# A transformer trunk's differential attention: one combining pass on VectorE and a turning product by a scaled diagonal

## What is computed

```python
def diff_attend(q, k, v, lam):
    b, h2, nq, _ = q.shape
    s = jnp.einsum('bhqd,bhkd->bhqk', q, k).astype(jnp.float32)
    p = jax.nn.softmax(s, axis=-1).reshape(b, h2 // 2, 2, nq, k.shape[2])
    w = p[:, :, 0] - lam * p[:, :, 1]
    return jnp.einsum('bhqk,bhkd->bhqd', w.astype(v.dtype), v)
```

## Time and profile before

| | |
|---|---|
| runs | 2911.39, 2913.27, 2911.05 us |
| median | 2911.39 us |
| span of the profiled execution | 2899.9 us |
| median less this span | 11.5 us |
| PE busy | 2795.9 us, 96% |
| DVE, ACT, POOL busy | 1636.0 (56%), 809.6 (28%), 305.8 us (11%) |
| mean granted clock of PE | 0.983 |

### The profile page before, as it was taken

How to read it: one execution, slowest core, us unless ns; L and a number is a source line. 1 busy time by engine, 2 the same in 40 slices (tenths; PEclk the granted TensorE clock), 3 DMA queues, 4 the chain that set the end, 5 groups by cost and what they waited for, 6 DMA issues and landing times.

```text
span 2899.9 us, 40732 instructions
## 1 busy us (share of the span) xinstructions
PE 2795.9 (96%) x15252; PEld 2522.6 (87%) x15252; DVE 1636.0 (56%) x2849; ACT 809.6 (28%) x1091; POOL 305.8 (11%) x293
## 2 busy tenths in 40 slices
PE   7999999999988999999999999999999988999998
PEld 6999999989744789999999899999997844788887
DVE  4676577658747567756676772222236758533334
ACT  4221122132346332211221322112223256322222
POOL 0000000031337100000000000000003336000000
PEclk9999999999997999999999999999999999999999
DMA  6333333321221113332332232111212311222222
GB/s 227 132 124 114 115 116 132 114 74 66 55 50 31 45 67 121 127 120 106 126 134 98 91 120 76 55 59 65 72 52 88 76 35 36 73 94 102 87 101 80
DMA packets 64419, 265.02 MB, mean 91 GB/s; under 512 B 9024, under 2 KB 11968, under 8 KB 54848
## 3 DMA queue, kind: packets, MB, share of 16 engines
q1 hardware_dynamic: 52800, 188.56, 18.7%
q0 software_dynamic: 11520, 75.11, 7.7%
HBM read 252.89 MB, written 2.10 MB: 88 GB/s over the span
## 4 chain that ended last, share of the span: by engine, by line
PE 91%; DVE 5%; ACT 2%; issue 2%; POOL 0%; DMA 0%; SPq 0%; DVEq 0%; ACTq 0%; POOLq 0%
PE ps L1682 82%; PE ps L2025 1%; PE ps L2007 1%; DVE nmax L1490 1%; PE ps L1959 1%; PE ps L1948 1%; PE ps L1710 1%; PE ps L1991 1%; PE ps L1951 1%; PE ps L1943 1%; DVE w_lo L1114 1%; DVE y_lo L1198 1%; ACT probs_t L1017 0%; PE ps L1917 0%; ACT e_sb L1003 0%
## 5 line engine op out<-in xcount | busy, mean ns | idle before, releaser
L1682 PE MATMUL ps<-y_hi,w_hi 128*128 128x384 f32 (+2 forms) x3184 | 902.7, 348 | 33.2 <-DVE y_lo L1198 17.4
L1682 PE MATMUL ps<-y_hi,w_lo 128*128 128x384 f32 (+2 forms) x3184 | 893.6, 345 | 0.0
L1682 PE MATMUL ps<-y_lo,w_hi 128*128 128x384 f32 (+2 forms) x3184 | 893.3, 345 | 0.0
L1682 PEld LDWEIGHTS ps<-y_hi,w_hi 128*128 128x128 f32 x3184 | 579.7, 189 | 70.3 <-DVE y_lo L1198 22.7
L741 ACT ACTIVATE w_hi<-w_raw 128x1024 fp32r<-128x1024 f32 (+1 forms) x290 | 327.0, 1128 | 1066.4 <-PE ps L1682 1058.9
L1682 PEld LDWEIGHTS ps<-y_lo,w_hi 128*128 128x128 f32 x3184 | 583.6, 189 | 24.8
L1682 PEld LDWEIGHTS ps<-y_hi,w_lo 128*128 128x128 f32 x3184 | 583.3, 189 | 23.7 <-issue 0.2
L1114 DVE TENSOR_TENSOR w_lo<-w_raw,w_hi 128x1024 fp32r<-128x1024 f32 (+1 forms) x290 | 386.4, 1333 | 323.0 <-ACT w_hi L741 319.7
L1129 DVE SCALAR_TENSOR_TENSOR mod_acc<-mod_raw,cact,mod_acc 128x256 f32<-128x256 f32 x896 | 360.0, 477 | 0.0
L1682 PE MATMUL ps<-h_hi,w_hi 128*128 128x384 f32 (+2 forms) x1254 | 355.6, 343 | 0.0
L1682 PE MATMUL ps<-h_lo,w_hi 128*128 128x384 f32 (+2 forms) x1254 | 353.4, 342 | 0.0
(11 more groups left out here) (232 smaller groups left out, 1903.0 us busy)
## 6 DMA issues: line engine op xcount, KB each, us to landing
w_raw<-in_w_up SPq DMA_DIRECT2D x176, 512.0 KB, 3.2
mod_raw<-in_w_mod POOLq DMA_DIRECT2D x64, 1024.0 KB, 5.1
w_raw<-in_w_down SPq DMA_DIRECT2D x64, 704.0 KB, 4.0
w_raw<-in_w_in SPq DMA_DIRECT2D x36, 512.0 KB, 3.2
mod_start<-in_w_mod SPq DMA_DIRECT2D x8, 1024.0 KB, 18.2
w_raw<-in_w_out SPq DMA_DIRECT2D x16, 512.0 KB, 3.2
stack<-qk_hi SPq DMA_DIRECT2D x48, 96.0 KB, 2.1
band<-in_rpb POOLq DMA_DIRECT2D x16, 224.0 KB, 6.7
```

Of the source, the lines that this page charges most:

```text
L1682: mm = pe.matmul(slot[s][:, at:at + b - a], w[s][:, k, :], r[:, k, a:b], start=(opens and n == 0), stop=(closes and n == 2))
```

## The change

Three things change for differential steps; neighbourhood steps keep their arithmetic.

First, the combination. The weights are p0/sum0 - lam * p1/sum1. They are now written as (p0 + c * p1) / sum0 with c = -lam * sum0 / sum1. DVE forms c in `nrsum` and makes the bracket in one scalar_tensor_tensor over both halves. POOL's two passes go.

Second, the division by sum0 moves into the turning. POOL makes a 128x128 diagonal (the identity times 1/sum0), and PE turns a block by an ordinary matmul with the block as weight and the diagonal as moving operand, where it was a transpose by the identity. The two diagonals lie in a free end of `w_lo`.

Third, in every odd iteration k the turned probabilities of a differential step are copied out of PSUM by DVE, and not by ACT.

Waits follow these edits: the semaphore `first_scaled` becomes `diagonal`, and DVE and POOL wait for older diagonals and turned tiles before they overwrite what these were made from.

```diff
+    diagonal = [place(f"diagonal{s}", [P, P], at=at_lo + 4 * (s * FG + DC) * P) for s in range(2)]
...
                     t.wait("sums_inverted")
-                    factor = nrsum[:, e - 1:e] if kind == "diff" else rsum[:, e:e + 1]
-                    factor = factor.to_broadcast([P, keys.stop - keys.start])
-                    probs = probs_of(steps, k, 1)
-                    pool.tensor_tensor(probs[:, keys], probs[:, keys], factor, ALU.mult).then_inc(sems["half_scaled"], 1)
                     if kind == "diff":
 
-                        t.wait("first_scaled")
-                        pool.wait_ge(sems["half_scaled"], scores_before(layer) // 2 + k + 1)
-                        first = probs_of(steps, k, 0)
-                        pool.tensor_tensor(first[:, keys], first[:, keys], probs[:, keys], ALU.add).then_inc(sems["probs"], 1)
+
+                        if k >= n_na + 2:
+                            pool.wait_ge(sems["turned"], turned_before(layer) + 2 * n_na + k - n_na - 1)
+                        pool.tensor_tensor(diagonal[k % 2][:, :], ident[:, :], rsum[:, e - 1:e].to_broadcast([P, P]),
+                                           ALU.mult).then_inc(sems["diagonal"], 1)
+                    else:
+                        factor = rsum[:, e:e + 1].to_broadcast([P, keys.stop - keys.start])
+                        probs = probs_of(steps, k, 1)
+                        pool.tensor_tensor(probs[:, keys], probs[:, keys], factor, ALU.mult).then_inc(sems["half_scaled"], 1)
...
-                            if s == 0:
+                            if s == 0 and turned[0] == "diff" and k % 2:
+                                t.skip("turned")
+                            elif s == 0:
                                 copy_probs(k, turned[2][s])
...
+                        if k >= n_na + 2:
+
+                            dve.wait_ge(sems["diagonal"], diff_before(layer) + k - n_na - 1)
+                        dve.wait_ge(sems["half_scaled"], na_before(layer) + min(k - 1, n_na))
+                        dve.reciprocal(rsum[:, e0:e0 + 2], esum[:, e0:e0 + 2]).then_inc(sems["sums_inverted"], 1)
+                        t.wait("sums_inverted")
+                        dve.scalar_tensor_tensor(nrsum[:, e0:e0 + 1], rsum[:, e0 + 1:e0 + 2], lam[:, 5:6], esum[:, e0:e0 + 1],
+                                                 ALU.mult, ALU.mult).then_inc(sems["stat"], 1)
+                        t.wait("stat")
...
-                    ins = dve.tensor_scalar(first, first, rsum[:, e0:e0 + 1], None, ALU.mult)
-                    ins.then_inc(sems["first_scaled" if kind == "diff" else "probs"], 1)
+                    if kind == "diff":
+
+                        ins = dve.scalar_tensor_tensor(first, probs_of(steps, k, 1)[:, keys], nrsum[:, e0:e0 + 1], first, ALU.mult, ALU.add)
+                    else:
+                        ins = dve.tensor_scalar(first, first, rsum[:, e0:e0 + 1], None, ALU.mult)
+                    ins.then_inc(sems["probs"], 1)
...
                     m = turned_at(steps, k)
-                    if m is None or steps[m][0] != "na":
+                    if m is None or steps[m][0] != "na" and k % 2 == 0:
                         return
...
+                    if kind == "diff":
+                        t.wait("diagonal")
...
-                        mm = pe.transpose(turn[:, P * n_key:P * n_key + P], probs[:, P * key:P * key + P], ident[:, :])
+                        block = probs[:, P * key:P * key + P]
+                        if kind == "diff":
+                            mm = pe.matmul(turn[:, P * n_key:P * n_key + P], block, diagonal[k % 2][:, :], start=True, stop=True)
+                        else:
+                            mm = pe.transpose(turn[:, P * n_key:P * n_key + P], block, ident[:, :])
```

More of the change, by code:

```diff
@@ L240 @@
     "v_turned", "v_ready0", "v_ready1", "band_raw", "band_step", "band_ready",
-    "scores", "neg_max", "exp", "stat", "sums_inverted", "probs", "half_scaled", "first_scaled", "na_hi", "na_lo", "turned", "probs_t", "pv", "head_out",
+    "scores", "neg_max", "exp", "stat", "sums_inverted", "probs", "half_scaled", "diagonal", "na_hi", "na_lo", "turned", "probs_t", "pv", "head_out",
     "head_sq", "head_sum", "head_sqrt", "head_rstd", "head_norm", "final", "out_stored",
@@ L281, in trunk @@
     w_hi = [place(f"w_hi{s}", [P, FG, P], F32R) for s in range(2)]
+    at_lo = cursor[0]
     w_lo = [place(f"w_lo{s}", [P, FG, P], F32R) for s in range(2)]
+    diagonal = [place(f"diagonal{s}", [P, P], at=at_lo + 4 * (s * FG + DC) * P) for s in range(2)]
     at_mod = cursor[0]
@@ L464, in diff_scores, with na_before, diff_before @@
         return 2 * sum(s[0] == "diff" for s in attention_steps(layer < LAYERS - 1))
+    def na_before(layer):
+        return sum(na_scores(n) for n in range(layer)) // 2
+    def diff_before(layer):
+        return sum(diff_scores(n) for n in range(layer)) // 2
     def na_scores(layer):
@@ L678, in mixer @@
                 steps = attention_steps(layer < LAYERS - 1)
+                n_na = sum(step[0] == "na" for step in steps)
                 for k, (kind, h, tiles, ctx, last) in enumerate(steps):
@@ L1496, in invert_sums @@
                     t.wait("exp", 2)
[L1497 to L1506, removed]
+                    if k < n_na:
+                        if k >= 2 or layer:
+                            dve.wait_ge(sems["half_scaled"], na_before(layer) + max(k - 1, 0))
+                            if layer:
+                                dve.wait_ge(sems["diagonal"], diff_before(layer))
                         dve.reciprocal(rsum[:, e0:e0 + 2], esum[:, e0:e0 + 2]).then_inc(sems["sums_inverted"], 1)
                         t.wait("sums_inverted")
+                    else:
[7 more added lines that the diff above has]
+                        t.wait("stat")
                 def scale_probs(k):
@@ L1528, in copy_second @@
                     m = turned_at(steps, k)
-                    if m is None or steps[m][0] != "na":
+                    if m is None or steps[m][0] != "na" and k % 2 == 0:
                         return
                     kind, h, tiles, ctx, last = steps[m]
-                    q = tiles[1]
-                    dve.wait_ge(sems["turned"], turned_before(layer) + 2 * (m + 1))
+                    q = tiles[-1]
+                    dve.wait_ge(sems["turned"], turned_before(layer) + sum(len(step[2]) for step in steps[:m + 1]))
                     if jobs_before(layer) + jobs_by(with_ctx, k):
@@ L2019, in transpose_probs @@
                     else:
-                        pe.wait_ge(sems["half_scaled"], scores_before(layer) // 2 + k + 1)
+                        pe.wait_ge(sems["half_scaled"], na_before(layer) + k + 1)
+                    if kind == "diff":
+                        t.wait("diagonal")
                     if tiles_turned:
```

## The result

| | before | changed |
|---|---|---|
| median of the runs beside each other | 2911.22 us | 2947.84 us |
| lowest, highest | 2909.39, 2913.27 | 2944.14, 2948.92 |
| ratio | | 1.0117 (95% interval 1.0097 to 1.0136) |
| span of the profiled execution | 2899.9 us | 2946.4 us |

A forecast was written before the change was run, and what follows sets the result against it. It took TensorE as the bound, 96% busy, with DVE and GpSimd bounding steps without value products. +8.4 us in the second mixer and +6.8 in the first gave +15.2 on 2911.4: 2927 us, range 2914 to 2944.

The forecast's parts named there:

- The product's price: Turning of differential blocks on TensorE: 0.23 us a product against 0.125 us a transpose, +0.63 us for six blocks.
- it is off every path: GpSimd's diagonal, estimated at 0.4 us, holds up nothing, being wanted two steps later.
- The wait for the copy: Turning after odd steps waits for DVE's copy, 3.4 us from second scores; stalls of 0.47 and 1.4 us in second-mixer head.
- The four steps with no head products before them: Second mixer, before its first head: a pair of steps takes 7.8 us against 7.46, +0.7 us in all.
- come out even: First mixer, six turned steps before the first head: no time added when stepped at full clock.
- The ends: Last steps of each mixer, to the output product: +1 us in the first mixer, +2.7 us in the second.
- rival A: Stretches without value products stay at 1.2 GHz, 1.2 us more in some ten turned steps, +12: 2939 us; chance 0.22.
- Rival B: No stall on the copy, only TensorE's own work added in the 21 full steps: 2920 us; chance 0.20.
- Rival C: Product costs what the transpose did, DVE's scaling shrinks in steps without products: about -8, 2903 us; chance 0.05.
- Rival D: Turning blocks cost 0.50 us instead of 0.23, 56 us beyond the forecast: 2983 us; chance 0.03.
- rival E: Whole kernel: the terms cancel and nothing measurable changes, 2911 us; chance 0.05.
- The base: Whole kernel: 11.5 us between the 2899.9 us span and the 2911.39 us median lie outside the span, unchanged.

The follow-up runs named there:

- nodiag_act: Changed kernel with identity transposes, ScalarE copying and no diagonal made, division by the first sum left out: 2911.05 us, ratio 0.9994 to the kernel before.
- product_act: Changed kernel, but ScalarE copies every differential turned tile; product and vector pass stay: 2924.23 us, ratio 1.0041 to the kernel before.
- before_again: The kernel before, unchanged, executed and traced once more: span 2919.7 us against 2899.9 in its first trace.
- before_product: The kernel before, with differential blocks turned by a matmul with the identity in place of the transpose: 2923.27 us, ratio 1.0034 to the kernel before.
- transpose_dve: Changed kernel with identity transposes, division by the first sum left out, DVE still copying in odd steps: 2927.44 us, ratio 1.005 to the kernel before.
- transpose_act: Changed kernel with identity transposes and ScalarE copying, division left out, diagonal still made: 2911.84 us, ratio 0.9995 to the kernel before.
- copy_first: Changed kernel with DVE's copy of a differential tile placed ahead of the vector pass in the same iteration: 2928.68 us, ratio 1.0055 to the kernel before.

## Why the prediction was wrong

The direction was right and the size was not: +15.2 forecast, some +34 measured, outside the range. The prices of the instructions held. What failed is the stepping: it let DVE be free at the start of each pair of steps and took TensorE at full clock throughout, and so made the waits for the copy too small. By stretches, from one turning to a later one, in us:

| stretch | before | changed | more | forecast |
|---|---|---|---|---|
| first mixer, six steps before the first head | 19.6 | 24.7 | +5.1 | 0 |
| its first head | 20.9 | 25.2 | +4.3 | +2.9 |
| its second head | 25.4 | 28.9 | +3.5 | +2.9 |
| its last steps, to `mix_out` | 25.6 | 29.7 | +4.0 | +1 |
| second mixer, four steps before the first head | 14.7 | 17.6 | +3.0 | +0.7 |
| its first head | 15.3 | 19.2 | +3.9 | +2.5 |
| its second head | 17.6 | 22.3 | +4.8 | +2.5 |
| its last steps, to `mix_out` | 18.0 | 22.7 | +4.7 | +2.7 |
| sum | | | +33.3 | +15.2 |

Every stretch grew by more than forecast. Of the 18 us that are missing, 7.3 lie before the first heads, 5.7 in the heads and 5.1 at the ends. (The stage lengths above give 33.5 us, from edges in tenths.)

*The product's price* held: 0.23 us a block forecast, 1.43 / 6 = 0.24 measured, two records each and 416 in all. *The vector pass* held: 1.01 us. *The diagonal* held at 0.40 us, but "it is off every path" failed in part: GpSimd's instruction stretches DVE's factor instruction from 0.22 to 0.46 us where they meet (15 of 40 steps in the changed kernel), and nodiag_act puts the diagonal with its waits at about 4 us in all, not far above what two traces differ by.

*The wait for the copy* was the right mechanism, in the right places (wait after odd iterations), and too small. Where DVE was free the step nearly held: forecast from the start of the second scores 3.4 us, measured from 2453.77 to 2457.39: 3.62. So the stalls of 1.4 us in the second mixer's heads measured 1.46 and 1.45. The stalls of 0.47 at step 16 and its like in the second head measured 1.19 and 1.20, and the head that was to take 17.8 us took 19.2. The largest error is in the steps without value products: in the second mixer "The four steps with no head products before them", at 7.8 us a pair, and in the first mixer the six that "come out even". It is the same error as at step 16. I let each pair begin with an idle DVE. In the trace it is not idle. The timeline of DVE before the turning at 2446.83:

```profile
2440.58 0.96 DVE L1503 TENSOR_REDUCE nmax<-ps 128x1 f32<-128x768 f32 x1 [2.42 <-PE ps L1971]
2441.45 1.01 DVE L1536 SCALAR_TENSOR_TENSOR e_sb<-e_sb,nrsum 128x768 f32<-128x768 f32 x1
2442.38 0.95 DVE L1503 TENSOR_REDUCE nmax<-ps 128x1 f32<-128x768 f32 x1
2443.25 0.15 DVE L1523 RECIPROCAL rsum<-esum 128x2 f32<-128x2 f32 x1
2443.44 0.46 DVE L1525 SCALAR_TENSOR_TENSOR nrsum<-rsum,lam,esum 128x1 f32<-128x1 f32 x1
2443.93 0.96 DVE L1503 TENSOR_REDUCE nmax<-ps 128x1 f32<-128x768 f32 x1
2444.80 1.01 DVE L1536 SCALAR_TENSOR_TENSOR e_more<-e_more,nrsum 128x768 f32<-128x768 f32 x1
2445.73 0.95 DVE L1563 COPY probs_t<-ps 128x768 f32<-128x768 f32 x1
2446.60 0.95 DVE L1503 TENSOR_REDUCE nmax<-ps 128x1 f32<-128x768 f32 x1
```

From 2440.58 on, DVE has no gap: the second maximum of step 14 had to wait for scores behind the late turning, and all that follows runs on to the copy's end. The turning of PE at steps 11, 12, 14, 15 and 16 (iterations k, as in DVE's order above):

```profile
2423.20 1.50 PE L2052 MATMUL ps<-diagonal,e_sb 128*128 128x128 f32 x12
...
2428.83 1.58 PE L2052 MATMUL ps<-diagonal,e_sb 128*128 128x128 f32 x12 [1.44 <-DVE probs_t L1563]
...
2437.11 2.72 PE L2052 MATMUL ps<-diagonal,e_more 128*128 128x128 f32 x12 [1.80 <-DVE probs_t L1563]
...
2440.83 1.57 PE L2052 MATMUL ps<-diagonal,e_sb 128*128 128x128 f32 x12
...
2446.83 1.58 PE L2052 MATMUL ps<-diagonal,e_sb 128*128 128x128 f32 x12 [1.19 <-DVE probs_t L1563]
```

The loop is turning, second scores, maximum, pass, maximum, inversion, maximum, pass, copy, and turning again: 1.43 + 0.65 + 0.87 + 0.93 + 0.87 + 0.41 to 0.65 + 0.87 + 0.93 + 0.95 + 0.15, about 8.2 us, and 2437.11 - 2428.83 = 8.28. From 2437.11 to 2446.83 it is 9.72, with turning at half clock (2.38 us). Before, two such steps took 7.46. In the four steps before the first head of the second mixer this gave +3.0 us (2423.20 to 2440.83) where I had +0.7. The kernel before had:

```profile
2392.14 0.82 PE L2025 MATMUL ps<-ident,e_sb 128*128 128x128 f32 x6
...
2406.81 1.50 PE L2025 MATMUL ps<-ident,e_sb 128*128 128x128 f32 x6
```

In the first mixer, from turning at 878.14 to 902.83 against 874.26 to 893.90, it gave +5.05 where I had none; the granted clock in that stretch is 0.69.

*The ends* failed in two terms. In the first mixer I had stalls of 1.1 us and took off 1.6 for a wait on ScalarE's copy. The trace has waits for DVE's copy of 2.03 and 1.42 us there, the second in the place of the one that I took off. In the second mixer the turning that follows a 2 us wait is at half clock, 2.58 us to the next work, and so are the value products behind it, 3.17 instead of 1.86; the stall of 0.9 that I had there for the copy did not come:

```profile
964.20 1.58 PE L2052 MATMUL ps<-diagonal,e_more 128*128 128x128 f32 x12 [2.03 <-DVE probs_t L1563]
...
2482.32 2.93 PE L2052 MATMUL ps<-diagonal,e_sb 128*128 128x128 f32 x12 [2.03 <-ACT hid_buf L1072]
```

*The clock* (rival A) came in half. The 1.2 GHz stretches, which my sum left out, did not vanish: the stages' clocks are 0.87 and 0.95, up from 0.80 and 0.91. Turning at half clock takes 2.4 to 2.6 us, which rival A priced rightly at 1.2 us more; it happens in six turnings of six blocks, where rival A had some ten. There was luck in the price: its 0.43 us a block was read from products over 64 columns, and the blocks here have 128.

*Rival B* (no stall) is excluded by the waits for the copy, 17.4 us in 14 cases, and by product_act: without the copy the kernel is 20 us faster in the stages. *Rival C* (faster) is excluded by the records; its mechanism exists, since the steps without products did fall to 3.35 us, and was worth nothing in time. *Rival D* is excluded by 0.24 us a block, *rival E* by the interval of the ratio.

*The base* was wrong in a detail. I took 11.5 us as lying outside the span. The changed kernel's profiled execution took 2948.10 us with a span of 2946.4, and before_again 2921.42 with 2919.7, so 1.7 us lie outside. If that holds for the first trace of the kernel before, its execution was some 10 us shorter than the median (an estimate: its own time is not on record). This moved no term.

## What to carry to other kernels

An instruction that is moved to an engine with free time costs what stands ahead of it in that engine's queue. Where another engine waits for it, follow the loop over as many iterations as its waits reach (two, here), starting from the state in which the loop leaves the queues, and not from idle engines. The position can matter more than the engine: the same copy placed ahead of the pass gave back 15 of its 16 to 20 us. A turning product must be compared with the transpose it replaces by its records: in FP32 it was two for one here, and folding a scale into it is dear where TensorE is the bound.

## What the runs showed of the hardware

- An FP32 product of a 128x128 weight with 128 columns leaves two records and takes 0.24 us at 2.4 GHz, the transpose of the same block one record and 0.125 us; at 1.2 GHz six products took 2.4 us (2437.11 to 2439.49), six transposes 1.14.
- Exchanging transposes for products, and nothing else, raised the granted clock of the stages from 0.80 and 0.91 to 0.91 and 0.98 (before_product), and the reverse exchange lowered it from 0.87 and 0.95 to 0.81 and 0.87 (transpose_dve). In before_product 9 of the 22 us that the products cost by themselves did not show up in the stages, while TensorE's idle time stayed at 33.1 and 32.4 us, so this is work that took less time and not idle time that was filled.
- A scalar_tensor_tensor of one element per partition on DVE takes 0.22 us alone. It takes 0.46 in all 96 cases of five traces (changed kernel, product_act, transpose_dve, transpose_act, copy_first) in which GpSimd's 0.40 us instruction over 128 columns started 0.04 or 0.05 us after it, and 0.22 in the 25 cases in which GpSimd's started 0.05 to 0.17 us after it.
